# A two-part bias and interleaved value products in an attention stage of a two-block layer kernel

## The reference

```
h    = rms_norm(x, norm_g);  proj = h @ w_in
q, k, v, z_att, u_shift, z_rwkv = split(proj)
att  = dilated_mixture_attention(q, k, v, pos) * silu(z_att)     # 16 heads of 64 channels
rwk  = rwkv7_time_mix(u_shift, z_rwkv, ...)                      # 16 heads of 64 channels
x    = x + concat([att, rwk]) @ w_out;  return rms_norm(x, final_g)
```

## Time and profile before

| | |
|---|---|
| time, median of 3 runs (lowest, highest) | 3447.58 us (3446.11, 3447.95) |
| the profiled execution: its own time, its span | 3449.15 us, 3447.2 us |
| busy share of the span: PE, DVE, ACT, POOL | 95%, 41%, 32%, 48% |
| share of PE in the chain that ended last | 80% |
| second attention: from the first scores to tile 212 | 3087.69 to 3245.5 us of the span |

### The profile page before, as it was taken

The page is one execution under the profiler, slowest core; times in us unless marked ns, Lnnn a source line. Parts: engine busy times, 40 slices in busy tenths (PEclk is TensorE's granted clock), DMA queues, the critical chain, the costliest instruction groups (busy, mean ns, idle before and its releaser), DMA issues.

```text
span 3447.2 us, 48580 instructions
## 1 busy us (share of the span) xinstructions
PE 3276.8 (95%) x18636; PEld 2530.9 (73%) x18636; DVE 1409.6 (41%) x2138; ACT 1117.4 (32%) x1470; POOL 1656.4 (48%) x1314
## 2 busy tenths in 40 slices
PE   5799998999889999999999969999999999999997
PEld 4688886878767878878777837777777777764586
DVE  8777783120142322222231054345345345455412
ACT  4344443233333323223333232233133223323321
POOL 2556652444547677777654424444344344341142
PEclk9899998999999999999999989999999999989999
DMA  3555556232212222222222222222122222232222
GB/s 131 155 149 160 161 166 172 94 135 100 86 60 76 84 85 85 80 81 83 85 73 86 97 106 94 74 83 89 68 95 89 71 81 89 80 108 70 98 92 94
DMA packets 122898, 341.60 MB, mean 99 GB/s; under 512 B 59408, under 2 KB 62480, under 8 KB 91664
## 3 DMA queue, kind: packets, MB, share of 16 engines
q1 hardware_dynamic: 122768, 339.67, 29.8%
HBM read 301.09 MB, written 33.82 MB: 97 GB/s over the span
## 4 chain that ended last, share of the span: by engine, by line
PE 80%; issue 10%; POOL 4%; DVE 4%; ACT 1%; DMA 0%; ACTq 0%; SPq 0%; POOLq 0%; DVEq 0%
PE bank L159 22%; PE bank L161 20%; PE bank L160 20%; POOL wlo L146 4%; PE bank L1327 3%; PE bank L1626 2%; PE bank L1627 2%; PE bank L1697 1%; PE bank L1014 1%; PE bank L1032 1%; PE bank L422 1%; ACT whi L140 1%; PE bank L421 1%; PE bank L433 1%; PE bank L407 1%
## 5 line engine op out<-in xcount | busy, mean ns | idle before, releaser
L146 POOL TENSOR_TENSOR wlo<-wraw,whi 128x512 fp32r<-128x512 f32 x912 | 1245.2, 1397 | 1479.1 <-ACT whi L140 1479.0
L159 PE MATMUL bank<-rhi,whi 128*128 128x512 f32 x3648 | 1493.9, 410 | 106.9 <-POOL wlo L146 38.7
L160 PE MATMUL bank<-rlo,whi 128*128 128x512 f32 x3648 | 1433.6, 393 | 0.0
L161 PE MATMUL bank<-rhi,wlo 128*128 128x512 f32 x3648 | 1433.2, 393 | 0.0
L159 PEld LDWEIGHTS bank<-rhi,whi 128*128 128x128 f32 x3648 | 691.7, 190 | 324.5 <-issue 90.4
L161 PEld LDWEIGHTS bank<-rhi,wlo 128*128 128x128 f32 x3648 | 691.8, 190 | 149.3
L160 PEld LDWEIGHTS bank<-rlo,whi 128*128 128x128 f32 x3648 | 693.1, 190 | 140.9 <-issue 11.3
L140 ACT ACTIVATE whi<-wraw 128x2048 fp32r<-128x2048 f32 x228 | 436.9, 1916 | 623.0 <-PE bank L161 478.0
L845 POOL TENSOR_TENSOR wraw<-wraw,vec 128x512 f32<-128x512 f32 x260 | 266.3, 1056 | 0.0
L753 DVE TENSOR_TENSOR ssum<-ssum,wk 128x512 f32<-128x512 f32 x30 | 21.6, 719 | 311.3 <-ACT wk L743 311.3
L743 ACT ACTIVATE wk<-bank 128x512 f32<-128x512 f32 x32 | 27.9, 870 | 236.7 <-PE bank L161 236.7
(11 more groups left out here) (356 smaller groups left out, 3289.1 us busy)
## 6 DMA issues: line engine op xcount, KB each, us to landing
wraw<-in_wall_dram SPq DMA_DIRECT2D x228, 1024.0 KB, 4.8
g<-in_bmat_dram SPq DMA_DIRECT2D x16, 512.0 KB, 5.6
g<-scr_e SPq DMA_DIRECT2D x128, 64.0 KB, 4.7
scr_a<-ssum SPq DMA_DIRECT2D x24, 256.0 KB, 2.1
g<-in_xp_dram SPq DMA_DIRECT2D x4, 1024.0 KB, 11.6
g<-in_cmat_dram SPq DMA_DIRECT2D x16, 256.0 KB, 4.3
scr_u<-wk SPq DMA_DIRECT2D x16, 256.0 KB, 5.9
scr_y<-wk SPq DMA_DIRECT2D x16, 256.0 KB, 2.2
```

What stands on the lines that cost most here:

```text
L146: ins = pool.tensor_tensor(wlo[:, slot, c], wraw[:, slot, c], whi[:, slot, c].bitcast(F32), ALU.subtract)
L159: pe.matmul(acc[slot][:, :], whk, rhi[:, k, :], start=(k == 0), stop=False)
L160: pe.matmul(acc[slot][:, :], whk, rlo[:, k, :], start=False, stop=False)
L161: ins = pe.matmul(acc[slot][:, :], wlk, rhi[:, k, :], start=False, stop=(k == KT - 1))
```

## The change

Two edits, and what they need:

1. The bias is split once into `bhi` (rounded to fp32r, ACT) and `blo` (the remainder, POOL), and `ident` is copied to an fp32r tile `idr` (ACT). Each block of scores then has one fp32 product and two fp32r products. The three live in slices 13 to 15 of `rhi` and `rlo`, which are free until the last heads.
2. `at_values` takes a pair of heads: it alternates between head 0 and head 1 for each of the four blocks, that is between the lower and the upper half of the array's columns. It runs in odd steps only, from `h = 3` on. A third buffer `p2` (where the fp32 bias was) holds the probabilities of a third head.

With it go: POOL's order (the subtraction for `blo` first, the `w2_lo` slices spread behind later turns), one `w2_hi` slice moved from before the attention to `h = 1`, the counts of `a_o`, and the removal of six unused semaphores.

```diff
+                act.activation(idr, ident[:, :], ACT.Copy)
+                act.activation(bhi, xt["bias"], ACT.Copy).then_inc(a_bh, 1)
-                w2_hi(act, range(0, 4))
+                w2_hi(act, range(0, 3))
...
+            if h == 0:
+                pe.wait_ge(a_bl, 1)
...
-                ins = pe.matmul(to, ident[:, :], xt["bias"][:, tri[b]:tri[b] + n], start=False, stop=True)
+                pe.matmul(to, idr, bhi[:, tri[b]:tri[b] + n], start=False, stop=False)
+                ins = pe.matmul(to, idr, blo[:, tri[b]:tri[b] + n], start=False, stop=True)
...
-            if h >= 2:
-                act.wait_ge(a_o, h - 1)
+            if h >= 3:
+                act.wait_ge(a_o, (h - 3) // 2 + 1)
...
-        def at_values(pe, h):
-            p, hd = h // 2, h % 2
-            pe.wait_ge(a_pa, 3 * h + 3)
-            pe.wait_ge(a_pd, h + 1)
-            if hd == 0:
-                pe.wait_ge(a_vc, p + 1)
-                pe.wait_ge(*((a_g, p) if p else (evac, N_W2 + 2)))
+        def at_values(pe, p):
+            pe.wait_ge(a_pa, 6 * p + 6)
+            pe.wait_ge(a_pd, 2 * p + 2)
+            pe.wait_ge(a_vc, p + 1)
+            pe.wait_ge(*((a_g, p) if p else (evac, N_W2 + 2)))
             for kb in range(4):
-                ins = pe.matmul(banks[1][hs_[hd], kb * P:T],
-                                at[f"vt{p % 2}"][:, kb * P + hd * CH:kb * P + (hd + 1) * CH],
-                                at[f"p{hd}"][:, p_tri[kb]:p_tri[kb] + (4 - kb) * P], start=(kb == 0), stop=(kb == 3))
+                for hd in range(2):
+                    ins = pe.matmul(banks[1][hs_[hd], kb * P:T],
+                                    at[f"vt{p % 2}"][:, kb * P + hd * CH:kb * P + (hd + 1) * CH],
+                                    at[f"p{(2 * p + hd) % 3}"][:, p_tri[kb]:p_tri[kb] + (4 - kb) * P],
+                                    start=(kb == 0), stop=(kb == 3))
...
-                if h >= 2:
-                    at_values(pe, h - 2)
+                if h % 2 and h >= 3:
+                    at_values(pe, (h - 3) // 2)
             pe.wait_ge(a_vc, 8)
             project(pe, N_W2, 0, range(0, 2), wait_r=96)
             at_transpose(pe, LAST)
-            at_values(pe, LAST - 1)
             project(pe, N_W2, 0, range(2, 4), wait_r=96)
-            at_values(pe, LAST)
+            at_values(pe, 7)
             project(pe, N_W2, 0, range(4, KT), wait_r=96)
...
         def at_pool(pool):
-            at_turn(pool, 0)
-            at_turn(pool, 1)
-            w2_lo(pool, range(0, 8))
-            for p in range(2, 8):
+            pool.wait_ge(a_bh, 1)
+            pool.tensor_tensor(blo, xt["bias"], bhi.bitcast(F32), ALU.subtract).then_inc(a_bl, 1)
+            for p in range(8):
                 at_turn(pool, p)
-                if p >= 3:
-                    w2_lo(pool, range(p + 5, p + 6))
-            w2_lo(pool, range(13, 14))
+                if p >= 2:
+                    w2_lo(pool, range((p - 2) * 2, min((p - 2) * 2 + 2, p + 6)))
+            w2_lo(pool, range(12, 14))
```

More of the change, by code:

```diff
@@ L118, in program @@
         ach = sem("ach")
-        pch = sem("pch")
         x_in = sem("x_in")
@@ L679, in program @@
         o_sq = sem("o_sq")
-        gate_x = sem("gate_x")
         x_out = sem("x_out")
@@ L818, in program @@
         f_nb = sem("f_nb")
[L819 to L822, removed]
         f_zs = sem("f_zs")
@@ L1562, in program @@
                "in1": g2[:, 0:3 * T], "sw1": g2[:, 3 * T:5 * T]}
+        flat = [r[:, 13:KT, :].rearrange("p k t -> p (k t)") for r in (rhi, rlo)]
+        bhi, blo, idr = flat[0][:, 0:1280], flat[1][:, 0:1280], flat[0][:, 1280:1280 + P]
+        a_bh, a_bl = sem("a_bh"), sem("a_bl")
+        at["p2"] = xt["bias"]
         def at_out(p):
@@ L1673, in at_part @@
             n = (4 - kb) * P
-            return at[f"p{h % 2}"][:, p_tri[kb]:p_tri[kb] + n], ab_[h % 2][bank][:, o:o + n]
+            return at[f"p{h % 3}"][:, p_tri[kb]:p_tri[kb] + n], ab_[h % 2][bank][:, o:o + n]
         def at_copy_dve(d, h):
-            if h >= 2:
-                d.wait_ge(a_o, h - 1)
+            if h >= 3:
+                d.wait_ge(a_o, (h - 3) // 2 + 1)
+            if h == 2:
+                d.wait_ge(a_bl, 1)
             d.wait_ge(a_pt, 3 * h + 3)
@@ L1682, in at_copy_act @@
         def at_copy_act(act, h):
-            if h >= 2:
-                act.wait_ge(a_o, h - 1)
+            if h >= 3:
+                act.wait_ge(a_o, (h - 3) // 2 + 1)
+            if h == 2:
+                act.wait_ge(a_bl, 1)
             for kb, n in ((2, 1), (3, 2), (1, 2)):
@@ L1710, in at_copy_v @@
             if p >= 2:
-                act.wait_ge(a_o, 2 * p - 2)
+                act.wait_ge(a_o, p - 1)
             act.activation(at[f"vt{p % 2}"], banks[0][:, :], ACT.Copy).then_inc(a_vc, 1)
         def at_gate(d, p):
-            d.wait_ge(a_o, 2 * p + 2)
+            d.wait_ge(a_o, p + 1)
             d.wait_ge(a_lz[p % 2], 16 * (p // 2) + 16)
@@ L1758, in at_act @@
                 if h == 1:
-                    w2_hi(act, range(4, 8))
+                    w2_hi(act, range(3, 8))
                 if h % 2 and h >= 5:
```

## The result

| | before | after |
|---|---|---|
| time, median (lowest, highest) | 3447.76 us (3446.11, 3448.03; 4 runs) | 3419.53 us (3417.93, 3425.87; 4 runs) |
| span of the profiled execution | 3447.2 us | 3418.9 us |
| start of the first scores, of the first product behind the last values | 3087.6, 3254.4 | 3086.6, 3226.1 |
| two steps (a pair of heads) at full clock | 18.97 us | 15.31 us |

The ratio is 0.992, with an interval of 0.9908 to 0.9932. The change gives 28.2 us where 30.6 were forecast. The time lies in the forecast's range (3408 to 3430), and all of that range is faster than before by more than the 7 us that can be told from no change.

The account below looks back on a forecast made before the run. PE, busy throughout the attention, was taken to bound the kernel. Terms 13.8 + 18.0 - 2.9 + 1.7 = 30.6 us off the median 3447.6 gave 3417.0 us, range 3408 to 3430.

Parts of the forecast that it names:

- bias, 16 heads: Attention scores on PE: fp32r bias products instead of fp32 gain 0.86 us per head, 13.8 us in all.
- values, 8 pairs: Attention values on PE: two heads run side by side on the array's halves, saving 2.25 us per pair, 18.0.
- wait for ACT's first copy: Before odd heads' scores from `h = 3` on: PE stands 0.42 us for ACT, 7 times, 2.9 us lost.
- clock: Heads 0 and 1 at 1.2 GHz: transposes come 3.5 us earlier, the rise comes with them, 1.7 us won.
- the fixed 0.2: Bias on PE: about 0.2 us beside streaming; plus 0.11 for weights, no gain at 128 columns against 0.33.
- The Trainium skill's figure for column tiles: Values on PE: 2.38 measured for three tiles, 1.59 estimated for two; 14.3 us gained in place of 18.0.
- What was said to be hidden: Attention: DVE's products, `blo` (3.1 us) on POOL and the pairs' loads (9.8 us, 3.4 to spare) cost PE nothing.
- The rival that the rise stays where it was: Attention start: clock rises at 3113.0 anyway, 1.7 us less gain, 3418.7 us; chance 0.18.
- one that never comes: Attention: PE's clock stays at 1.2 GHz for the whole stage, 106 us more, 3523 us; slower has chance 0.02.

Follow-up runs that it names:

- Experiment 1: The kernel before with the two-part fp32r bias alone, values as before: 3434.83 us, ratio to before 0.9962.
- Experiment 2: The changed kernel with the value loops exchanged, head 0's four products ahead of head 1's: 3432.75 us, ratio to before 0.9951.
- Experiment 3: The changed kernel with ACT's first copy of the transposes moved ahead of the last two exponentials: ratio to before 0.9925, span 3416.1 us.
- Experiments 4 and 6: 16 extra fp32r products of 512 columns ahead of the first scores: 4 on the changed kernel, 3414.19 us; 6 on the kernel before, 3443.58 us.
- experiment 11: The changed kernel with scores of blocks 3, 2, 1 first, then their biases, then block 0: 3408.59 us, ratio to before 0.9882.

## Why the prediction was right, and where it was not

The time and all but one of the terms held. The sum again, with what it measured, in spans:

| term | forecast | measured |
|---|---|---|
| bias, 16 heads | +13.8 | +14.6 |
| values, 8 pairs | +18.0 | +18.4 |
| wait for ACT's first copy | -2.9 | -2.7 |
| clock | +1.7 | -3.9 |
| ahead of the stage | 0 | +1.0 |
| not assigned | | +0.9 |
| sum | +30.6 | +28.3 |

*Bias: right, a little small.* From the start of the first scores of an odd head to the values in the same step were 6.97 us before and are 3171.52 - 3165.46 = 6.06 after: 0.91 per head, not 0.86. At 512 and 384 columns the distances are the forecast's 0.66 and 0.55. At 256 they are 0.43, and at 128 the fp32r pair costs 0.27, not the same 0.33: I had charged the fixed 0.2 in full on top of the 0.11 of one narrow instruction, and the two distances are 0.16 and 0.11. Experiment 1 finds the 0.91 again by itself.

*Values: right.* 2.3 us for a pair, which is one head's time. The instructions of the two halves start 10 ns apart and last as long as alone. Experiment 2 shows that it is the order of issue that brings 12.4 of the 18.4; the rest is what PE's own look ahead finds. The Trainium skill's figure for column tiles ("TensorE: Matmul & The Clock Gate", Measured speedup vs the span model), worked out to 2.8 us per pair as an estimate (4.60 / 1.59 is 2.9), is not borne out for two tiles of 64 columns in fp32: the row says 2.3. The strict order of starts that the Trainium skill states (same page, The mechanism) is not either: in experiment 2 a product starts ahead of earlier ones on the other half.

*The wait: right in size, in one place fewer.* Six odd heads stand 0.38 each, from `h = 5` on (6 * 0.38 = 2.28, all of the idle time of the second stretch); counted by the step it is 0.45 (6.95 against 7.41 - 0.91); what makes up the other 0.07 is not shown. `h = 3` falls into the low clock, where PE comes later than the copy. Experiment 3 removes exactly this 0.45.

*What was said to be hidden was hidden.* `blo` and the turns of loaded pairs, in the timeline of POOL after:

```profile
3074.61 2.89 POOL L1774 TENSOR_TENSOR rlo<-wk,rhi 128x1280 fp32r<-128x1280 f32 x1
3077.46 2.00 POOL L1611 TENSOR_TENSOR wk<-wk 128x1024 f32<-128x1024 f32 x1
3151.64 2.00 POOL L1611 TENSOR_TENSOR wk<-wk 128x1024 f32<-128x1024 f32 x1 [9.97 <-DMA wk<-scr_a]
```

`blo` took 2.89 (3.1 forecast), and the first turn ended 7 us before the first scores. The turn of a later pair ends at 3153.64, 4.9 us before its scores at 3158.51 (3.4 forecast). DVE's last product of head 8 ended 3.3 us before its transposes.

*The clock: wrong, the step that failed.* The prediction tied the rise to the first transposes, "if the rise comes with them, 1.7 us more are won". They did come 5.0 us earlier, but the rise went to the second set, at 3119.8. So the stage had 33.1 us at half pace against 25.3 before; half of the 7.8 is 3.9 lost, in place of 1.7 won. The rival that the rise stays where it was had the sign of the error but not its size, and no rival had a later rise short of one that never comes. Experiments 4 and 6 show that this term is more than the whole of the miss: with the clock raised ahead of the stage in both kernels, 29.8 us are saved where the other terms forecast 28.9. That half of a low stretch is lost is an estimate. Beside experiments 6 and 4, which run the same steps at full clock, the low stretches of before and after cost 11.8 and 14.9 us rather than 12.7 and 16.6 (with the waits taken off that only those two kernels have); the clock's term is then -3.1, and 0.1 is left not assigned.

*Some luck in the time.* By the table the clock missed by 5.6 us, and the other rows by 3.3 the other way, of which 1.9 (ahead of the stage, not assigned) are no terms of the forecast. The time came within 2.4 us because they cancel in part.

*What places the rise* stays open. All positions here are the timelines', which give starts 0.2 earlier than the chain. In the two profiles whose first transposes start at 3106.1 (experiment 1) and 3110.2 (before), it comes 2.3 and 2.9 us behind them. In the five in which they start at 3103.3 to 3105.1 (after, twice, and experiments 2, 3 and 11), it comes 3.6 to 4.2 us behind the start of the second set. Each time ten transposes in a row go before it; which set it is can't be told from PE's program, as experiment 1 shows. Ten transposes take 2.15 us to the next start at 0.50, and 3164.48 - 3163.36 = 1.12 at 1.00, so the trace doesn't bear out the Trainium skill's sentence that in transpose mode the full clock doesn't engage (same page, Part 4).

The 1.0 us ahead of the stage is less than what the first scores move by between two profiles of one kernel (3086.6 and 3084.8 for after), so no cause is sought for it.

## What to carry to other kernels

On a stage where PE is busy throughout, count the distances between starts: they gave each term of this change but the clock's to a tenth of a us per head, and they also show the 0.2 us at each change of array shape, whose removal by mere reordering was worth nearly as much as cheaper arithmetic. Products that use different column halves run fully side by side only if they are issued in turn, and taking work from between a producer and its reader uncovers a wait, which is to be priced by the producer's queue. Earlier work at the low clock is no promise of an earlier rise: forecast the clock as a term of its own with both signs, and try a few gapless products on all rows where a stage begins at 1.2 GHz.

## What the runs showed of the hardware

- Sixteen fp32 instructions on two halves of the array's columns, issued in turn, took 2.3 us, as eight on one half did; the two of a couple started about 10 ns apart.
- Extra work of 5.1 us ahead of the stage shortened the profiled execution by 8.0 us (the median by 5.3), since the clock was back at 2.4 GHz 1.9 us behind its start, where the stage's own work, with PE 100% busy, took 33.1. Over the six profiles with such work the lag was 1.9 to 4.2 us, for fp32 as for fp32r.
- A change of array shape cost 0.19 us at full clock: four fewer per head made a pair 1.55 us shorter (experiment 11).
- DVE's two products of 0.55 us took 2.39 us while POOL subtracted fp32 tiles (experiment 1), and 2.37 in before; with POOL idle they took 0.55. That the two are linked is read from this coincidence alone.
